# A two-layer transformer on one core: who prepares the first two weight tiles, and where three small products stand

## The reference

```python
def diff_attn_layer(x, norm_g, w_in, w_out, ..., subln_g, lambda_init, cos, sin, cid):
    h = rms_norm(x, norm_g)                       # a mean of squares over the 2048 features
    q, k, v, gate = jnp.split(h @ w_in, 4, axis=-1)
    q = partial_rope(q.reshape(B, L, 16, 128), cos, sin)
    k = partial_rope(k.reshape(B, L, 16, 128), cos, sin)
    lam = exp(sum(lq1 * lk1)) - exp(sum(lq2 * lk2)) + lambda_init
    o = diff_attention(q, k, v.reshape(B, L, 8, 256), lam, cid)    # softmax minus lam * softmax, per head
    o = rms_norm(o, subln_g) * (1.0 - lambda_init)                 # a mean of squares per head
    return x + (o.reshape(B, L, 2048) * silu(gate)) @ w_out
```

## Time and profile before

| | before |
|---|---|
| median of 3 runs | 2648.57 us (2648.28 to 2649.2) |
| the profiled execution | 2649.55 us |
| its span in the profile | 2647.7 us |
| TensorE busy | 2591.1 us, 98% |
| GpSimd busy | 1902.3 us, 72% |
| ScalarE busy | 1225.4 us, 46% |
| VectorE busy | 978.4 us, 37% |
| mean granted TensorE clock | 0.989 of full |

### The profile page before, as it was taken

The page is one execution under the profiler, slowest core; times in us unless marked ns, Lnnn a source line. Parts: engine busy times, 40 slices in busy tenths (PEclk is TensorE's granted clock), DMA queues, the critical chain, the costliest instruction groups (busy, mean ns, idle before and its releaser), DMA issues.

```text
span 2647.7 us, 54457 instructions
## 1 busy us (share of the span) xinstructions
PE 2591.1 (98%) x22558; PEld 2442.5 (92%) x22558; DVE 978.4 (37%) x1361; ACT 1225.4 (46%) x1504; POOL 1902.3 (72%) x786
## 2 busy tenths in 40 slices
PE   7999999999999999999999999999999999999998
PEld 7899999999999999999898989999998898998986
DVE  5444444316666330314354544314371120120211
ACT  4344444555666654535353444345453343443443
POOL 5666677676666787757574757688698888888886
PEclk8999999999999999989999999999999999999999
DMA  5454455454444566545353535466566566666664
GB/s 187 138 156 143 144 147 156 129 175 138 135 145 142 151 184 213 151 120 163 115 160 109 161 112 160 128 191 209 158 177 188 178 189 203 186 187 190 185 189 151
DMA packets 119614, 426.51 MB, mean 161 GB/s; under 512 B 12784, under 2 KB 17008, under 8 KB 119152
## 3 DMA queue, kind: packets, MB, share of 16 engines
q1 hardware_dynamic: 114560, 416.55, 52.8%
q10 hardware_dynamic: 4848, 6.82, 0.8%
HBM read 419.12 MB, written 4.19 MB: 160 GB/s over the span
## 4 chain that ended last, share of the span: by engine, by line
PE 92%; DVE 4%; ACT 3%; issue 1%; DMA 0%; POOL 0%; SPq 0%; DVEq 0%; ACTq 0%; POOLq 0%
PE ps L315 15%; PE ps L218 15%; PE ps L220 15%; PE ps L227 15%; PE ps L241 5%; PE ps L249 5%; PE ps L243 5%; PE ps L1893 3%; PE ps L306 3%; PE ps L302 2%; PE ps L301 2%; PE ps L1183 2%; ACT wh L199 1%; PE ps L840 1%; PE ps L1785 1%; PE ps L1787 1%
## 5 line engine op out<-in xcount | busy, mean ns | idle before, releaser
L2886 POOL TENSOR_TENSOR wl<-raw,wh 128x1024 fp32r<-128x1024 f32 x782 | 1902.1, 2454 | 728.2 <-ACT wh L199 727.1
L199 ACT ACTIVATE wh<-raw 128x2048 fp32r<-128x2048 f32 x391 | 748.2, 1914 | 647.0 <-DMA raw<-weights 173.9
L218 PE MATMUL ps<-hh,wh 128*128 128x256 f32 (+1 forms) x3056 | 752.1, 285 | 3.5 <-DVE hl L351 2.3
L220 PE MATMUL ps<-hl,wh 128*128 128x256 f32 (+1 forms) x3056 | 749.0, 284 | 0.0
L218 PEld LDWEIGHTS ps<-hh,wh 128*128 128x128 f32 x3056 | 577.3, 189 | 8.6 <-issue 4.2
L220 PEld LDWEIGHTS ps<-hl,wh 128*128 128x128 f32 x3056 | 577.9, 189 | 0.1
L227 PE MATMUL ps<-hh,wl 128*128 128x256 f32 (+1 forms) x3056 | 398.2, 283 | 0.0
L227 PEld LDWEIGHTS ps<-hh,wl 128*128 128x128 f32 x3056 | 379.9, 188 | 0.3 <-POOL wl L2886 0.2
L315 PE MATMUL ps<-hh,wh 128*128 128x256 f32 x896 | 223.8, 290 | 0.0
L315 PE MATMUL ps<-hl,wh 128*128 128x256 f32 x896 | 215.6, 281 | 0.0
L241 PE MATMUL ps<-wh,gh 128*128 128x512 f32 x512 | 203.0, 397 | 0.0
(11 more groups left out here) (438 smaller groups left out, 3338.2 us busy)
## 6 DMA issues: line engine op xcount, KB each, us to landing
raw<-weights SPq DMA_DIRECT2D x782, 512.0 KB, 3.6
xT<-tokens SPq DMA_DIRECT2D x4, 544.0 KB, 7.1
spill<-xT ACTq DMA_DIRECT2D x1, 2048.0 KB, 13.4
xT<-spill ACTq DMA_DIRECT2D x1, 2048.0 KB, 10.3
out<-arena SPq DMA_DIRECT2D x4, 512.0 KB, 3.2
C<-consts SPq DMA_DIRECT2D x1, 2000.0 KB, 13.9
arena<-lora ACTq DMA_DIRECT2D x4, 384.0 KB, 3.2
arena<-rows ACTq DMA_DIRECT2D x1, 1024.0 KB, 6.6
```

The source lines that it names most:

```text
L199: nc.scalar.activation(wh[:, m % 2, :, :].rearrange("p a b -> p (a b)"), raw[:, 2 * (m % 2):2 * (m % 2) + 2, :, :].rearrange("p a b c -> p ...
L218: nc.tensor.matmul(acc[0:m, 0:n], wh[:, slot, kt, 0:m], rh[:, kt, 0:n], start=(kt == kts[0]), stop=False)
L220: nc.tensor.matmul(acc[0:m, 0:n], wh[:, slot, kt, 0:m], rl[:, kt, 0:n], start=False, stop=False)
L2886: nc.gpsimd.tensor_tensor(wl[:, s // 2, h, :], raw[:, s, :, :], wh[:, s // 2, h, :].bitcast(F32), ALU.subtract)\
```

## The change

1. ScalarE squares one column of constants before the first tokens land. It makes the high parts of quarters 0 to 2 only, in steps of two feature blocks (`h0` to `h5`), and rounds weight tile 0 after quarter 0 and tile 1 after quarter 2. All four quarters of squares follow in one go.
2. VectorE makes the high part of quarter 3 itself, between the remainders of quarters 1 and 2. After the fourth remainder it makes the weight remainders of tiles 0 and 1 (four instructions), and only then adds the squares up.
3. GpSimd's loop begins with tile 2, once the four remainders are there.
4. TensorE's order: piece 4 of tile 0 goes behind pieces 0 and 1 of tile 1; the column sums go from behind piece 3 to ahead of piece 3 of tile 2; the product that spreads the factors goes from ahead of piece 2 to ahead of piece 0 of tile 3; in heads 1 to 7 the ones-product goes from ahead of piece 2 to ahead of piece 3 of tile 0.

```diff
@@ start_act
+            act.wait_ge(eps_set, 7)
+            nc.scalar.activation(st[:, 63:64], eps[:, 3:4], ACT.Square)
             act.wait_ge(p_in, 16)
-            for k in range(4):
+            for k in range(3):
                 act.wait_ge(x_in[k], 16)
                 for kt in range(4 * k, 4 * k + 4):
                     ins = nc.scalar.activation(hh[:, kt, :], xT[:, kt, :], ACT.Copy, scale=p("a", kt))
-                ins.then_inc(A.sem, A.step(f"h{k}"))
-                if k == 1:
+                    if kt % 2:
+                        ins.then_inc(A.sem, A.step(f"h{kt // 2}"))
+                if k == 0:
                     round_weights(act, "a", 0)
             round_weights(act, "a", 1)
-            start_squares(range(0, 2))
+            for k in range(4):
+                if k == 3:
+                    act.wait_ge(x_in[3], 16)
                 nc.scalar.activation(squares_a[:, k], xT[:, 4 * k:4 * k + 4, :], ACT.Square)\
                     .then_inc(A.sem, A.step(f"q{k}"))
@@ start_dve
+            def rest(k):
                 for kt in range(4 * k, 4 * k + 4):
+                    if k < 3 and kt % 2 == 0:
+                        dve.wait_ge(A.sem, A.at(f"h{kt // 2}"))
+                    elif k == 3 and kt == 12:
+                        dve.wait_ge(V.sem, V.at("hi"))
                     ins = nc.vector.scalar_tensor_tensor(out=hl[:, kt, :], in0=xT[:, kt, :], scalar=p("a", kt),
...
+            rest(0)
+            rest(1)
+            dve.wait_ge(x_in[3], 16)
+            for kt in range(12, KT):
+                ins = nc.vector.tensor_scalar(hh[:, kt, :], xT[:, kt, :], p("a", kt), None, ALU.mult)
+            ins.then_inc(V.sem, V.step("hi"))
+            rest(2)
+            rest(3)
+            for s in range(4):
+                h = slice(8 * (s % 2), 8 * (s % 2) + 8)
+                dve.wait_ge(hi_done, s // 2 + 1)
+                nc.vector.tensor_tensor(wl[:, s // 2, h, :], raw[:, s, :, :], wh[:, s // 2, h, :].bitcast(F32),
+                                        ALU.subtract)\
+                    .then_inc(lo_done, 1)
@@ start_pe
-            for t, k in ((0, 0), (0, 1), (0, 2), (0, 4), (0, 3), (1, 0), (1, 1), (0, 5), (1, 2), (1, 3), (1, 4),
+            for t, k in ((0, 0), (0, 1), (0, 2), (0, 3), (1, 0), (1, 1), (0, 4), (0, 5), (1, 2), (1, 3), (1, 4),
@@ attn_a_pe
-                            if (t, piece) == (2, 4):
+                            if (t, piece) == (2, 3):
                                 pe.wait_ge(cp_in, 16)
                                 factor_a.pe_sum(pe)
-                            if (t, piece) == (3, 2):
+                            if (t, piece) == (3, 0):
                                 factor_a.pe_all(pe)
                                 lam_pe(pe)
...
-                            if piece == 2:
+                            if piece == 3:
                                 attn_a_sum(pe, i - 1)
@@ attn_a_act
-                    if i == 0 and t == 0:
-                        start_squares(range(2, 4))
-                    elif i == 0:
+                    if i == 0 and t:
                         factor_a.act(act)
                         lam_act(act)
@@ gpsimd
-            pool.wait_ge(SI["v"].sem, SI["v"].at("l3"))
-            with pool.Fori(0, N_TILES // 2) as i:
+            pool.wait_ge(lo_done, 4)
+            with pool.Fori(1, N_TILES // 2) as i:
```

More of the change, by code:

```diff
@@ L642, in dve_early @@
                 early.dve(eng, 15)
-        SI = phase("start", a="h0 h1 h2 h3 q0 q1 q2 q3",
-                   v=f"l0 l1 l2 l3 a0 a1 a2 f1 s{KT - 1} rs ck cm sk sm qs ns")
+        SI = phase("start", a="h0 h1 h2 h3 h4 h5 q0 q1 q2 q3",
+                   v=f"l0 l1 hi l2 l3 a0 a1 a2 f1 s{KT - 1} rs ck cm sk sm qs ns")
         squares_a = arena[:, ARENA - 16 * NT:ARENA].rearrange("p (k a n) -> p k a n", k=4, a=4)
@@ L701, in start_act @@
                     ins = nc.scalar.activation(hh[:, kt, :], xT[:, kt, :], ACT.Copy, scale=p("a", kt))
-                ins.then_inc(A.sem, A.step(f"h{k}"))
-                if k == 1:
+                    if kt % 2:
+                        ins.then_inc(A.sem, A.step(f"h{kt // 2}"))
+                if k == 0:
                     round_weights(act, "a", 0)
             round_weights(act, "a", 1)
-            start_squares(range(0, 2))
-        def start_squares(quarters):
-            A = SI["a"]
-            for k in quarters:
+            for k in range(4):
+                if k == 3:
+                    act.wait_ge(x_in[3], 16)
                 nc.scalar.activation(squares_a[:, k], xT[:, 4 * k:4 * k + 4, :], ACT.Square)\
@@ L717, in start_dve @@
             lam_products(dve)
-            for k in range(4):
-                dve.wait_ge(A.sem, A.at(f"h{k}"))
+            def rest(k):
                 for kt in range(4 * k, 4 * k + 4):
+                    if k < 3 and kt % 2 == 0:
+                        dve.wait_ge(A.sem, A.at(f"h{kt // 2}"))
+                    elif k == 3 and kt == 12:
+                        dve.wait_ge(V.sem, V.at("hi"))
                     ins = nc.vector.scalar_tensor_tensor(out=hl[:, kt, :], in0=xT[:, kt, :], scalar=p("a", kt),
```

## The result

| | before | after |
|---|---|---|
| median of the runs | 2648.81 us (2648.28 to 2649.2, 4 runs) | 2620.35 us (2614.95 to 2623.99, 4 runs) |
| profiled execution: time, span | 2649.55, 2647.7 us | 2614.95, 2613.2 us |
| mean granted clock | 0.989 | 0.997 |

The ratio is 0.9891, with a 95% interval of 0.9873 to 0.9909: 24 to 34 us less. Forecast were 26.2 us less, 2622.4 us. The profiled execution of after is the fastest of its runs.

A forecast was written before the change was run, and what follows sets the result against it. TensorE's stream (busy 98% of the span), plus its idle time and lower-clock work, was taken to bound the kernel. Gains 4.0 + 17.4 + 4.8 = 26.2 us off 2648.57 gave 2622.4 us, range 2619 to 2630.

The forecast's parts named there:

- The start: Up to tile 1's end: first product at 9.8 to 11.2, end at 27.7; gain 4.0 us, between 2.9 and 5.3.
- The sums: Column sums in tile 2: squares added by 29, asked for at 30.4, so TensorE's 6.73 us wait goes.
- the squares meet GpSimd: Rival at the column sums: three additions wait for GpSimd, TensorE waits 3.9 us, about 2626 us; chance 0.12.
- Keys and queries: Head 0's key and query chain: ends at about 51, asked for at 53.1, so the 3.5 us wait goes.
- the first rival: Key and query chain stays 17.1 us long, ends 1.3 us late, up to 4.5 more lost: about 2628; chance 0.12.
- The stretch: From tile 1's end to tile 0 of head 1: 69.60 us falls to about 51.5, gain 17.4 us.
- The ones-product: Heads 1 to 7: sum ready before TensorE asks, 0.68 us less per head, gain 4.8 us.
- The sum: Whole kernel: gains of 4.0, 17.4 and 4.8 make 26.2 us, giving 2622.4 us.
- given back: Rival after head 0: gain lost later in a stretch set by weight transfers, 2645 us; chance 0.03.
- slower by the clock: Rival at the start: two gaps keep TensorE at the lower clock through tile 6, 2655 us; chance 0.02.

The follow-up runs named there:

- after_again: The kernel after, unchanged, run again later: 2623.41 us, ratio 0.9893.
- after_third: The kernel after, unchanged, run a third time: 2623.27 us, ratio 0.9907.
- after_sums_back: The kernel after with column sums and spread factors back at their old pieces of tiles 2 and 3: 2629.32 us, ratio 0.993.
- after_ones_back: The kernel after with the ones-product of heads 1 to 7 back ahead of piece 2: 2627.86 us, ratio 0.9917.
- wl_only: The kernel before with only the weight remainders of tiles 0 and 1 on VectorE, GpSimd's loop from tile 2: 2645.39 us, ratio 0.9995.
- squares_wl: The kernel before with squares in one go and weight remainders of tiles 0 and 1 on VectorE: 2636.04 us, ratio 0.9951.
- after_act_hi: The kernel after with the high parts of quarter 3 back on ScalarE: 2621.47 us, ratio 0.9902.
- after_pool_rest: The kernel after with the weight remainders of tiles 0 and 1 back on GpSimd: 2627.13 us, ratio 0.9928.
- squares_only: The kernel before with only the four quarters of squares made in one go by ScalarE: 2639.86 us, ratio 0.9968.

## Why the prediction was right, step by step

**The start.** Three instructions of ScalarE and four of VectorE in after:

```profile
8.25 1.91 ACT L199 ACTIVATE wh<-raw 128x2048 fp32r<-128x2048 f32 x1 [1.42 <-DMA raw<-weights]
...
25.11 1.91 ACT L199 ACTIVATE wh<-raw 128x2048 fp32r<-128x2048 f32 x1 [0.94 <-DMA raw<-weights]
...
27.72 0.18 ACT L889 ACTIVATE arena<-ps 128x16 f32<-128x16 f32 x1 [0.70 <-PE ps L306]
```

```profile
12.68 1.17 DVE L734 TENSOR_SCALAR hh<-xT,P 128x272 fp32r<-128x272 f32 x4
13.77 3.38 DVE L726 SCALAR_TENSOR_TENSOR hl<-xT,P,hh 128x272 fp32r<-128x272 f32 x8
17.07 4.62 DVE L741 TENSOR_TENSOR wl<-raw,wh 128x1024 fp32r<-128x1024 f32 x4
21.61 5.05 DVE L751 TENSOR_TENSOR arena<-arena 128x1088 f32<-128x1088 f32 x5
```

The weights landed at 8.25, near the estimate of 7.9 from the bytes, and TensorE's first product ran at 10.31, inside 9.8 to 11.2. The high parts cost 0.29 each, under the bound of 0.36; `l3` came at 17.15, forecast 17.1. The clock fell at 12.8, in the first of the two gaps, and rose again at 19.7, forecast 20. Half microseconds of after around both:

```profile
12.50:13.00 0.50, 0.18 (x1) 0.18 (x2) 0.50 (x3) 0.50 (x3) 0.00 (x0) 0.85 0.98 401
...
19.50:20.00 0.50, 0.50 (x5) 0.50 (x4) 0.50 (x1) 0.50 (x2) 0.00 (x0) 0.82 1.17 139
```

Tile 1 ended at 27.72, forecast 27.7. The hit to two hundredths is luck in part: in after_again the clock rose at 20.2 and in after_third at 21.0, and this point lay at 27.64 and 28.11. Two variants with the same start lay further off: 26.00 where the clock never fell (after_sums_back), 28.52 where it was low from 11.2 to 21.4 (after_ones_back).

What earns the 4.0 us is another matter than the first product. The same point in wl_only and in squares_wl, which keep ScalarE's old order and begin at 12.81 and 12.99:

```profile
28.79 0.16 ACT L876 ACTIVATE arena<-ps 128x16 f32<-128x16 f32 x1
```

```profile
28.46 0.18 ACT L876 ACTIVATE arena<-ps 128x16 f32<-128x16 f32 x1 [1.10 <-PE ps L306]
```

So 2.9 of the 4.0 us come with the weight remainders on VectorE, the clock of these executions included. The first product 2.7 us earlier than in squares_wl brings 0.7 by the end of tile 1, because the last quarter comes hardly earlier, as the prediction says, and because the lower clock lasted 6.8 us in after and 3.4 in squares_wl.

Three readings of the clock in the prediction are off; none moves the forecast. By the rows of half a microsecond the clock fell at 11.3 and not 11.2, and came back at 48.9 and not 48.6. A rise at 21.5 gives an end at 28.1 by the prices used, not 28.5, so the lower bound of the gain was 3.3 and not 2.9.

**The sums.** The four weight remainders took 4.62 us and ended at 21.7, forecast 22.0; each is 1.22 long in the records, as forecast, but they overlap. The additions took 5.05 and ended at 26.66, the lower end of 26.7 to 31.3. I had taken 29, with two additions beside GpSimd. GpSimd began at 27.10 instead of 25.8, for the most part since ScalarE waited 0.94 us for the weights of tile 2 (the row at 25.11), which the prediction had called not late. So the additions missed GpSimd by 0.4 us, and by 0.3 and 0.1 in after_again and after_third. Up to 30.5, when TensorE asks for the sums, a later end costs nothing, so the rival "the squares meet GpSimd" was 3.8 us away; with TensorE early, in after_act_hi, they met and 0.5 us was left. after_pool_rest shows the meeting in full, 14.43 us for five.

**Keys and queries.** The step at which the working was off. I expected the end at 51, from two gaps of GpSimd, and a slack of 2.1 us. Three of the chain's instructions, all on VectorE:

```profile
37.92 2.88 DVE L962 TENSOR_TENSOR arena<-arena 32x544 f32<-32x544 f32 x1
...
43.67 0.71 DVE L967 TENSOR_TENSOR arena<-arena 32x544 f32<-32x544 f32 x1
...
50.10 2.80 DVE L983 TENSOR_TENSOR arena<-arena 32x544 f32<-32x544 f32 x1
```

The first addition of the chain began at 37.9, where the forecast had 37.3, and only one of its instructions ran at its price alone, 0.71 us, in GpSimd's gap from 43.06 to 43.90; the second gap, 49.49 to 49.93, fell inside an instruction that took 2.09 us and spared nothing (2.10 in before). The chain took 15.0 us and ended at 52.90. TensorE asked at about 53.4. The slack was 0.5 us, and as much in after_again and after_third, where the same instruction met the gap. In after_sums_back and squares_wl no addition meets a gap, the chain takes 17.1 us and TensorE waits 3.5. So the first rival (chance 0.12) missed by half a microsecond. Its price was about right in sum, 1.3 of wait and up to 4.5 of clock forecast, 3.5 and 2.0 measured.

**The stretch.** 17.4 us forecast, from 69.60 to 51.5 with the small products at 1.7. Measured 18.0, to 51.56; the small products cost 51.56 - 49.71 = 1.85, and the reference head itself shrank by 0.80, which the subtraction from 50.51 had not seen.

**The ones-product.** 0.68 a head forecast, 0.80 measured (50.51 - 49.71), 5.6 us in all. TensorE's timeline there in after, to be laid beside the earlier trace rows:

```profile
75.49 0.29 PE L302 MATMUL ps<-hl,wh 128*128 128x272 f32 x1
75.61 0.62 PE L315 MATMUL ps<-arena,C 128*128 128x272 f32 x2
75.87 0.49 PE L301 MATMUL ps<-hh,wh 128*128 128x272 f32 x1
```

The hole ahead of the pair went from 0.81 to 0.12, which was the forecast's term. The pair itself also went from 0.36 to 0.26, which was not in it.

**The sum.** 26.2 forecast, 26.8 measured up to tile 65. Which edit bears how much, by the markers: squares in one go and the remainders on VectorE together 14.1 (squares_wl), the ones-product 5.6, the new start order 0.7 at the end of tile 1 (27.72 against 28.46). That leaves 6.4 us for the column sums and factors moved up, an estimate by difference; after_sums_back has 5.5 for them in its stretch. The 0.7 us are less than what the clock does to the start from one execution to the next, and no run has the new start order alone. The parts hang together: alone, the squares in one go took away the wait of 6.7 us, but the wait for the remainders grew from 2.1 to 4.9.

**Given back later?** No: -26.8 at tile 65 and -26.6 at tile 156. The rival "given back" is refuted, and so is "slower by the clock": in none of the three traces of after was the clock still low past 21.0 us in the start.

**What it did not see.** Nothing in the forecast allowed for 8 us of scatter by the clock in one stage. It started from an execution of before in which the stage ran at the lower clock, and so assumed the same of after; the fastest run of after, 2614.95, lies outside the range of 2619 to 2630 for that reason. The median, 2620.35, lies 2 us from the forecast, and that it is so near is partly luck too: the three comparisons give from 24.0 to 28.5 us for the same change.

## What to carry to other kernels

Before a trace's total is compared with another's, align both by an instruction that recurs in each: what a change gives shows within its stage, and luck shows as a step elsewhere. A wait that is taken away can make another longer, so ask what a freed engine will run beside; here the earlier squares alone removed a wait of 6.7 us for the sums and lengthened the one for the remainders from 2.1 to 4.9, and the subtractions on VectorE took most of that one away too. An engine that starts earlier need not end earlier: TensorE's first product came 2.7 us sooner, the end of tile 1 only 0.7. Long runs of small products may be paid for at the lower clock; with large ones between them they were not.

## What the runs showed of the hardware

- **The clock fell under a TensorE that never idled.** In the logits stage the profile has TensorE busy for 100% of the window in both traces, at 1.00 once and at 0.64 once. The stage takes 19.30 us in one and 12.96 in the other. It fell in 11 of the 12 traced executions without interleaving, for 13.7 or 17.1 us, and in neither of the two with it. Which property of those products (4 rows, few columns, fp32 in pairs) does it is open.
- **Short spells of the lower clock elsewhere**, 3.4 us each, came between 604 and 631 us and between 1881 and 1913 us in some executions and not in others of the same kernel. Their cause was not tried. That they, the start and the logits stage make up the scatter of both kernels (before 2639 to 2653 us, after 2615 to 2626) fits the traces and is not shown, since few of the runs have one.
- **VectorE beside GpSimd.** An addition or multiplication of 32x544 took 0.71 us alone and 2.08 to 2.93 beside GpSimd, five additions of squares 5.05 and 14.43. This goes both ways: GpSimd's weight remainders became so late in squares_only that TensorE waited 4.9 us for them, where it waited 2.1. Most of the chain's instructions, 0.71 us of work, paid about the length of one of GpSimd's subtractions (9.42 us for four). By the Trainium skill ("SBUF — State Buffer", Who interferes with whom) the two engines take turns on a shared port by whole instructions; the trace agrees, with these numbers.
- **A shuffle is spared.** STREAM_SHUFFLE of 32x544 took 0.78 us at 47.16 in after, in the midst of GpSimd's work, where the instructions of the same size before and after it took 2.91 and 2.09. In before, at 64.99 us, it is 0.77 between 2.92 and 2.10.
